# Tails of the shrinking projections as seven half-size products, with their weight sums formed in the third pair

## The reference

```python
x = x + (1.0 + g2)[:, None, :] * conv_ffn(h, ff_w_up[i], ff_conv_w[i], ff_conv_b[i], ff_w_down[i])
...
def rms_norm(x, gain):
    y = xf * lax.rsqrt(jnp.mean(xf * xf, axis=-1, keepdims=True) + RMS_EPS)
```

## Time and profile before

| | us |
|---|---|
| median of 3 runs (lowest, highest) | 2300.97 (2299.34, 2303.53) |
| the profiled execution | 2300.7 |
| its span in the trace | 2298.7 |
| PE busy in it | 2268.2 (99%) |
| DVE busy | 1730.2 (75%) |
| ScalarE busy | 548.3 (24%) |
| mean granted clock of PE | 0.998 |

### The profile page before, as it was taken

The page is one execution under the profiler, slowest core; times in us unless marked ns, Lnnn a source line. Parts: engine busy times, 40 slices in busy tenths (PEclk is TensorE's granted clock), DMA queues, the critical chain, the costliest instruction groups (busy, mean ns, idle before and its releaser), DMA issues.

```text
span 2298.7 us, 45516 instructions
## 1 busy us (share of the span) xinstructions
PE 2268.2 (99%) x18014; PEld 2038.0 (89%) x18014; DVE 1730.2 (75%) x3683; ACT 548.3 (24%) x1388; POOL 184.0 (8%) x296
## 2 busy tenths in 40 slices
PE   8999999999999999999999999999999999999999
PEld 4478999656799997999999799998799998999998
DVE  5866997478579876769986589968769976667883
ACT  2232110027221102213211432212432212213220
POOL 0000011000001010011100011000012100001100
PEclk9999999999999999999999999999999999999999
DMA  6434777751557766468966288674469874456752
GB/s 244 158 129 161 257 276 256 275 186 47 177 202 275 258 257 220 161 218 242 270 234 233 111 233 263 214 262 139 138 202 288 280 260 163 146 173 180 209 179 77
DMA packets 136448, 474.26 MB, mean 206 GB/s; under 512 B 15296, under 2 KB 17472, under 8 KB 135872
## 3 DMA queue, kind: packets, MB, share of 16 engines
q1 hardware_dynamic: 95136, 338.80, 42.2%
q0 software_dynamic: 41120, 132.73, 19.1%
HBM read 470.42 MB, written 1.05 MB: 205 GB/s over the span
## 4 chain that ended last, share of the span: by engine, by line
PE 93%; DVE 5%; ACT 1%; issue 1%; DMA 0%; DVEq 0%; ACTq 0%
PE pair L688 53%; PE bank L688 38%; PE bank L1170 1%; ACT h L1689 1%; PE bank L1000 0%; DVE arena L2955 0%; DVE arena L2995 0%; DVE arena L2991 0%; DVE arena L2363 0%; DVE rstd L2163 0%; DVE arena L3366 0%; PE bank L1111 0%; DVE arena L2438 0%; DMA x<-x_in_dram 0%; DVE h L2172 0%
## 5 line engine op out<-in xcount | busy, mean ns | idle before, releaser
L688 PE MATMUL pair<-arena,ring 128*128 128x128 f32 (+1 forms) x2840 | 389.6, 294 | 3.8 <-issue 2.0
L688 PEld LDWEIGHTS pair<-arena,ring 128*128 128x128 f32 x2840 | 363.6, 192 | 20.0 <-issue 3.6
L688 PE MATMUL bank<-arena 128*128 128x128 f32 (+4 forms) x3172 | 367.0, 278 | 1.9 <-DVE arena L2591 0.8
L688 PEld LDWEIGHTS bank<-arena 128*128 128x128 f32 (+3 forms) x3172 | 348.0, 185 | 16.1 <-issue 6.7
L688 PE MATMUL pair<-arena 128*128 128x128 f32 (+5 forms) x3706 | 340.2, 264 | 2.5 <-DVE arena L2310 1.0
L688 PEld LDWEIGHTS pair<-arena 128*128 128x128 f32 (+4 forms) x3706 | 312.3, 170 | 31.5 <-issue 19.6
L688 PE MATMUL bank<-arena,ring 128*128 128x128 f32 (+1 forms) x2548 | 308.0, 277 | 0.5 <-DVE arena L2363 0.3
L688 PEld LDWEIGHTS bank<-arena,ring 128*128 128x128 f32 x2548 | 295.9, 192 | 3.0 <-DVE arena L2363 0.7
L688 PE MATMUL pair<-h,ring 128*128 128x128 f32 (+1 forms) x2048 | 294.2, 299 | 1.5 <-ACT h L1689 0.9
L688 PEld LDWEIGHTS pair<-h,ring 128*128 128x128 f32 x2048 | 269.9, 192 | 14.6 <-ACT h L1689 1.9
L2758 DVE CUSTOM_DVE_ANT_0 adat<-adat,crow,cols 128x1024 f32<-128x1024 f32 x192 | 243.1, 1277 | 48.0 <-DMA adat<-adaw_dram 48.0
(11 more groups left out here) (320 smaller groups left out, 2460.0 us busy)
## 6 DMA issues: line engine op xcount, KB each, us to landing
ring<-stream_dram SPq DMA_DIRECT2D x638, 512.0 KB, 5.0
adat<-adaw_dram POOLq DMA_DIRECT2D x192, 512.0 KB, 5.3
ring<-stream_dram POOLq DMA_DIRECT2D x80, 256.0 KB, 6.7
arena<-gmrows_dram POOLq DMA_DIRECT2D x1, 2560.0 KB, 11.2
arena<-gmrows_dram POOLq DMA_DIRECT2D x5, 512.0 KB, 9.1
arena<-cmpw_dram POOLq DMA_DIRECT2D x1, 2112.0 KB, 8.6
x<-x_in_dram SPq DMA_DIRECT2D x2, 512.0 KB, 4.5
arena<-mem_in_dram SPq DMA_DIRECT2D x1, 1024.0 KB, 8.8
```

What stands on the lines that cost most here:

```text
L688: return nc.tensor.matmul(out, lhsT, rhs, start=start, stop=stop)
```

## The change

- `tail_pair` replaces the halves in the tail: seven products of K/2 matmuls. The first five give all that the first half of the tokens needs; the last two (the mixed ones, for the second half alone) come last. Their banks are those of the tail's two groups, one late bank, and both banks of the second and of the third pair, for which PE waits.
- `norm_sum(norm, 0)` stands in the sixth product, in front of its matmul j = 5.
- DVE forms four more sums of weights for the tail, in the loop of the third pair. Its modulation tiles, which stood alone in that loop, come behind the four sums and in front of the pair's combination. The first three sums wait for the fourth, fifth and sixth product of the third pair (`down_read`), the fourth for the pair's end (`mm_done`).
- `early_tail` and `late_tail` are the additions to `x`; the latter stands inside `normalise` of the first half, at k = 1 and k = 5. ScalarE copies the tail's first product and squares the second half at k = 5 in place of after k = 7.
- `norm_sum(norm, 1)` stands at k = 4 in place of 3 behind a shrinking projection, where the next one runs in halves.
- In the last norm, the gain's product over the first six tiles comes after `normalise` of the first half.

```diff
@@ plan, tiles_of
+                if kind == "tail":
+                    lin.tail = (at - lin.K * len(ns), group + len(places) - TAIL)
+            counts[grows] += len(lin.pairs) + (not grows)
-            if kind == "pair":
+            if kind in ("pair", "tail"):
@@ names
+                for p in range(len(lin.pairs)):
+                    DOWN_READ.append([("down_read", n_read + r + 1) for r in range(3)] + [("mm_done", lin.g0 + p + 1)])
+                    n_read += 3
+                DOWN_READ.append([("mm_done", lin.g0 + lin.groups)] * 4)
+        def tail_places(g):
+            return [USED[g][0], USED[g + 1][0], LATE[0], *USED[g - 2], *USED[g - 1]]
@@ TensorE, seven
+                def tail_pair(t, g):
+                    own = down_own(name)
+                    places = tail_places(g)
+                    def product(n, stationary, move, free=None, before=None):
+                        for j in range(half_k):
+                            if before is not None and j == 5:
+                                before()
+                            ins = mm(banks[places[n]][:, 0:P], stationary(j), move(j), j == 0, j == half_k - 1)
+                            if j == 0 and free is not None:
+                                release(ins, True, free)
+                        return ins
+                    bank_free(g)
+                    bank_free(g + 1)
+                    product(0, lambda j: tile(t + j), lambda j: moving(2 * j)[:, HALVES[0]], t
+                            ).then_inc(sem("half_done"), 1)
+                    product(1, lambda j: tile(t + 3 * half_k + j), lambda j: sums[:, 3, j, :]
+                            ).then_inc(sem("half_done"), 1)
+                    product(2, lambda j: tile(t + half_k + j), lambda j: moving(2 * j + 1)[:, HALVES[0]]
+                            ).then_inc(sem("half_done"), 1)
+                    pe.wait_ge(sem("freed_dve"), FREER[g - 2][1])
+                    pe.wait_ge(sem("down_summed"), 4 * (lin.pair0 + len(lin.pairs)) + 2)
+                    product(3, lambda j: own[2][:, j, :], lambda j: sums[:, 2, j, :]).then_inc(sem("half_done"), 1)
+                    pe.wait_ge(sem("down_summed"), 4 * (lin.pair0 + len(lin.pairs)) + 4)
+                    product(4, lambda j: own[1][:, j, :], lambda j: sums[:, 1, j, :], t + 2 * lin.K
+                            ).then_inc(sem("half_done"), 1)
+                    pe.wait_ge(sem("freed_dve"), FREER[g - 1][1])
+                    product(5, lambda j: own[3][:, j, :], lambda j: moving(2 * j + 1)[:, HALVES[1]], None,
+                            lambda: norm_sum(norm, 0)).then_inc(sem("mm_done"), 1)
+                    product(6, lambda j: own[0][:, j, :], lambda j: sums[:, 0, j, :]).then_inc(sem("mm_done"), 1)
-                        for i in range(TT):
-                            for at in range(len(ns)):
...
+                        tail_pair(t, g)
@@ h_ready
-                late_k = 3 if PLAN[SOURCE[norm]].kind == "S" else 4
+                late_k = 4
@@ ScalarE, squares
+                if lin.kind == "S":
+                    act.wait_ge(sem("half_done"), HALF[name] + 1)
+                    nc.scalar.copy(ebuf[:, len(lin.pairs) % 2, 7, :], banks[tail_places(lin.tail[1])[0]][:, 0:P]
+                                   ).then_inc(sem("first_copied"), 1)
...
+                        if i == 0 and lin.kind == "S" and k == 5:
+                            last_squares(1)
@@ VectorE, residual
                     for r in range(4):
-                        if p + 1 < len(lin.pairs):
-                            down_weights(name)
-                        if between is not None and r < 3:
+                        down_weights(name)
+                        if between is not None and r < 3 and p + 1 < len(lin.pairs):
                             between(3 * p + r)
+                    for r in range(3 if between is not None and p + 1 == len(lin.pairs) else 0):
+                        between(3 * p + r)
                     e = ebuf[:, p % 2]
                     link(combined(lin.g0 + p, e))
+                def early_tail():
+                    e = ebuf[:, len(lin.pairs) % 2]
+                    p4, p2, p7, p6 = (banks[b][:, 0:P] for b in tail_places(lin.tail[1])[1:5])
+                    dve.wait_ge(sem("first_copied"), FIRST[lin.tail[1]])
+                    corner = chained(plus_row(C, e[:, 7:8, :]))
+                    dve.wait_ge(sem("half_done"), HALF[norm] + 2)
+                    fourth = chained(plus(E, x[:, E, HALVES[0]], p4))
+                    dve.wait_ge(sem("half_done"), HALF[norm] + 3)
+                    after(corner)
+                    plus(C, x[:, C, HALVES[0]], p2).then_inc(sem("x_half"), 1)
+                    add_squares(C - 1, slice(0, TOK), C)
+                    dve.wait_ge(sem("half_done"), HALF[norm] + 4)
+                    mixed = chained(V.tensor_tensor(e[:, 4, :], p7, e[:, 7, :], ALU.add))
+                    after(max(fourth, mixed))
+                    row = chained(plus_row(E, e[:, 4:5, :]))
+                    dve.wait_ge(sem("half_done"), HALF[norm] + 5)
+                    after(row)
+                    plus(E, x[:, E, HALVES[0]], p6).then_inc(sem("x_half"), 1)
+                    add_squares(C, HALVES[0], C + 1)
+                    sixth = chained(plus(C, x[:, C, HALVES[1]], p6))
+                    return sixth, chained(plus(E, x[:, E, HALVES[1]], p6))
+                def late_tail(k):
+                    if k == 1:
+                        dve.wait_ge(sem("mm_done"), lin.tail[1] + 1)
+                        after(late[0])
+                        late[0] = chained(plus(C, x[:, C, HALVES[1]], banks[tail_places(lin.tail[1])[5]][:, 0:P]))
+                    if k == 5:
+                        fifth = banks[tail_places(lin.tail[1])[6]][:, 0:P]
+                        dve.wait_ge(sem("mm_done"), lin.tail[1] + 2)
+                        after(max(late))
+                        plus(C, x[:, C, HALVES[1]], fifth).then_inc(sem("freed_dve"), 1)
+                        plus(E, x[:, E, HALVES[1]], fifth).then_inc(sem("freed_dve"), 1)
+                        add_squares(C, HALVES[1], C + TAIL + 1)
...
+                normalise(norm, gain, 0, late_part if lin.kind == "F" else late_tail)
+                if norm == "final":
+                    gained(0, DK - TAIL)
+                    dve.wait_ge(sem("sq_done"), SQUARES[norm] + DK + TAIL)
+                    gained(DK - TAIL, DK)
                 normalise(norm, gain, 1)
@@ VectorE, down_weights
-                    dve.wait_ge(sem("down_read" if r < 3 else "mm_done"), 3 * (q - 1) + r + 1 if r < 3 else DOWN_GROUP[q - 1])
+                    signal, value = DOWN_READ[q - 1][r]
+                    dve.wait_ge(sem(signal), value)
```

More of the change, by code:

```diff
@@ L524, in build @@
                 SOURCE[f"mix2_{i}"] = f"cdown{i - 1}"
+        ROOTS, SQUARES, ADDED, TAILS, HALF = {}, {}, {}, {}, {}
+        n_root = n_square = n_added = n_tail = n_half = 0
+        for name in NORMS:
+            ROOTS[name], SQUARES[name], ADDED[name], TAILS[name] = n_root, n_square, n_added, n_tail
+            HALF[name] = n_half
+            n_half += 0 if name in WHOLE else 5 if PLAN[SOURCE[name]].kind == "S" else TAIL
+            n_root += 1 if name in WHOLE else TT
+            n_square += DK if name in WHOLE else DK + TAIL
+            n_added += 0 if name in WHOLE else DK - TAIL - 1 + TT
+            n_tail += 0 if name in WHOLE else TAIL
         SPREADS = {}
@@ L552, in build @@
                 n_sums += len(lin.ktiles)
-        DOWN_GROUP = [lin.g0 + p + 1 for lin in PLAN.values() if lin.kind == "S" and not lin.grows
-                      for p in range(len(lin.pairs))]
+        DOWN_READ, n_read = [], 0
+        for lin in PLAN.values():
+            if lin.kind == "S" and not lin.grows:
+                for p in range(len(lin.pairs)):
+                    DOWN_READ.append([("down_read", n_read + r + 1) for r in range(3)] + [("mm_done", lin.g0 + p + 1)])
+                    n_read += 3
+                DOWN_READ.append([("mm_done", lin.g0 + lin.groups)] * 4)
         UP_PAIRS = [(t, g, lin.name) for lin in PLAN.values() if lin.kind == "S" and lin.grows
@@ L572, in down_own @@
             return gm_out_own(name) if name.startswith("gm_out") else downW[name != "down0"]
+        TAIL_GROUPS = [lin.tail[1] for lin in PLAN.values() if lin.kind == "S" and not lin.grows]
+        def tail_places(g):
+            return [USED[g][0], USED[g + 1][0], LATE[0], *USED[g - 2], *USED[g - 1]]
         FIRST = {}
         for g, place in enumerate(USED):
-            if len(place) > 1:
+            if len(place) > 1 or g in TAIL_GROUPS:
                 FIRST[g] = len(FIRST) + 1
@@ L829, in seven @@
                 t, g = lin.tile0, lin.g0
[L831 to L837, removed]
                 grows = lin.grows
@@ L1692, in squares @@
                             last_squares(1)
-                    if i == 0 and (shift is None or lin.kind == "S"):
```

(11 more changed lines are left out.)

19 lines of the change are left out of this document (8 added, 11 removed).

## The result

The changed kernel takes 2316.13 us (median of 4 runs, 2315.23 to 2317.16); the kernel before took 2301.73 beside it (2299.34 to 2303.53). The ratio is 1.0065, 95% interval 1.005 to 1.0079: 14.4 us slower, with 82 matmuls fewer. The profiled execution has a span of 2314.9 us, 16.2 more than before; 1.4 of that had already gone before the first tail, nearly all of it in the first 19 us, where the two programs do the same. So this part is no effect of the change.

What follows compares the result with a forecast made beforehand. TensorE, 93% of the chain, was taken as the bound. Removed matmuls give at most 18.3 us, but waits and seams bring the sum to +8.05: 2309.0 us, own range 2305.6 to 2314, wider range 2299.5 to 2318.

Steps and rivals of the forecast that it cites:

- rival 4: In the five tails with tiles, TensorE's waits bring its clock down: +8.5 us, 2317.5 in total; chance 0.15.
- five tails, DVE's work late: Tiles behind the fourth sum delay combination and additions: 2.46 us saved, 4.5 waited, plus 2.1 each, +10.5 us.
- five tails, the clock: In the five tails with tiles, no clock loss was counted in the forecast's sum: 0 us.
- `gm_out0` with `cup0`: Tail with two tiles and the seam behind it: -1.79 + 0.5 + 0.45 = -0.8 us.
- `gm_out3` with `cup3`: Tail without tiles and the seam behind it: -1.79 + 0.45 = -1.3 us.
- `cdown3` and the end: Tail without tiles saves 2.46 us; the later gain's product at the kernel's end costs 1.3: -1.2 us.
- `hg_f`, `mla_q`: Starts of these two linears: later `norm_sum` costs 0.45 us in the first, later input 0.4 in the second.
- `nsa_in`, behind `down0`: Start of the linear behind this tail: no loss was forecast, 0 us.
- rival 1: Quick refills: both tile refills in the five tails land in 3.4 us, no change, 2300.5; chance 0.2.
- The cover behind `norm_sum`: In the tail, 17 matmuls (3.80 us) behind `norm_sum`, plus its own 0.45, suffice to cover the first `h` tile.
- Rival 2: Combination in the five tails starts before T0 + 6.8 (T0: tail's first matmul), so TensorE never waits: 2286.2; chance 0.08.
- The seams: From tail to next linear: `norm_sum` at k = 4 costs 0.45 us at `cup0`, `cup3`, `hg_f`; `mla_q` 0.4; end 1.3.

Runs made afterwards that it cites:

- Experiment 4: Changed kernel with ten more matmuls, their result unused, in front of `norm_sum` in the five tails with tiles: 2305.19 us, ratio 1.0017.
- experiment 5: Changed kernel with four more matmuls, their result unused, in front of `norm_sum` in the five tails with tiles: 2306.65 us, ratio 1.0026.
- experiment 1: Changed kernel with the third pair's modulation tiles and their loads left out (27 of 192): 2286.94 us, ratio 0.9937.
- experiment 7: Changed kernel, third pair's tiles spread: one behind each of the first three sums, two behind the combination: 2286.59 us, ratio 0.9937.
- experiment 9: Kernel with tiles spread and k = 3, the gain's product over six tiles put before the last norm's first half: 2285.81 us, ratio 0.9934.
- experiment 6: Changed kernel with three more matmuls in front of the sixth product in the five tails with tiles: 2314.22 us, ratio 1.0055.
- experiment 8: Changed kernel with the third pair's tiles spread and the second half's `norm_sum` back at k = 3: 2286.47 us, ratio 0.9936.
- late tiles, old tail: Kernel before the change, with VectorE holding the third pair's tiles until TensorE has ended that pair: 2317.81 us, ratio 1.0067.

## Why the prediction came out as it did

The sign and the place were right, and the cause that was forecast is a real one, but it is only a part of the loss: 2316.1 is 7.1 us above 2309 and outside the forecast's own range of 2305.6 to 2314. It lies in the wider range only because that one took in rival 4 (2317.5). From the offsets and the start of each tail in the two traces, in us:

| step | forecast | measured |
|---|---|---|
| five tails, DVE's work late | +10.5 | +7.0 |
| five tails, the clock | 0 | +9.05 |
| `gm_out0` with `cup0` | -0.8 | -0.45 |
| `gm_out3` with `cup3` | -1.3 | -0.79 |
| `cdown3` and the end | -1.2 | -1.6 |
| `hg_f`, `mla_q` | +0.85 | +1.2 |
| `nsa_in`, behind `down0` | 0 | +0.4 |
| sum | +8.05 | +14.8 |

**The step that failed** is the clock, taken at nothing in the forecast's sum and kept apart as rival 4 at 0.15. What a fall would cost was right (1.7 us each, measured 1.51 to 2.65), and the waits came much as that rival had them: 0.62 to 1.33 us, then 2.33 to 2.64. What failed is the argument against it, that the waits at the start "came one after the other, with little work between". The row was misread. Between the wait of 7.1 us and that of 2.1 us PE worked for 3.59 us:

```profile
7.10 3.59 PE L688 MATMUL bank<-h,cst 128*128 128x256 f32 x8 [7.10 <-DVE h L2842]
```

That is more than the 1.4 us between the two waits of a tail, so the start spoke for rival 4 and not against it. It was weak evidence all the same. The profile after shows the same two waits and a granted clock of 1.00 in both stretches of the earlier trace rows, though PE is 1.3 us later by their end than before; so the clock shown for the first 20 us can't be taken as it stands. Experiment 4 shows the price in the time: 10.9 us, of which the rows of the five tails account for 9.05. The Trainium skill ("TensorE: Matmul & The Clock Gate", "What's actually happening") has the array's clock halved when PE has been idle. The five falls agree with it. That PE has stood still is not enough by itself here: in experiment 5 waits of 1.32 and 1.74 us brought no fall.

**DVE's lateness was mis-sized**, +1.4 us a tail for 2.1. The pieces behind the combination were right: in `cdown1` 3.76 us to the first addition (3.77), 2.16 to the last (2.15), 0.60 to `norm_sum` (0.70). The combination itself came at 10.56 to 10.81 in four tails, and at 11.45 in `down1`, where I had 11.26. In `cdown1` the second landing is the reason, 4.5 us where I took 5.1. So the truth lay between the forecast and rival 1. This error and that of the clock have opposite signs, so that the total is no further off is partly luck; experiment 4, with the clock held, came out at 2305.2, 3.8 below the forecast of a kernel with no clock in it.

**The cover behind `norm_sum`** was right: from there to the next linear it is 4.25 us in experiments 1 and 7 (0.45 + 3.80 in the forecast) and 4.34 behind the wait of experiment 4, and PE does not wait in it. Rival 2 gave 2286.2 and said that it needs some tiles ahead of the last sum. Experiment 7 does that and took 2286.59.

**The seams.** I put all 0.45 us behind `gm_out0` and `gm_out3` down to k = 4. They cost 0.82 each, and behind `gm_out3` k = 3 gives nothing back: the input is late by itself. The tail of `gm_out3` saves 1.61 us (14.74 to 13.13), where I had 1.79. Behind `cdown1` the 0.45 was right: PE's wait for the sums (1.03 us) ended 11.76 us after the start of `hg_f`, now it ends at 12.22, and at 11.88 with k = 3. The rest of the 0.7 there comes later in `hg_f`, and that part varies between kernels with the same seam, so I don't put it down to the change. At the end the reciprocal came 2.66 us after DVE's last addition began, where it was 1.60: +1.1 for my +1.3, of which experiment 9 takes back 0.59. The 0.4 in `nsa_in` I had at nothing. From its start to `down1`'s tail it is 422.91 us before and 423.32 after, but 422.91 to 422.98 in experiments 1, 4, 6, 7, 8 and 9, which have the same seam, and 423.44 in experiment 5. So the seam alone doesn't cost it, and its cause is open.

## What to carry to other kernels

When a stage is given new work on a side engine, look at what stands behind it in that engine's order, and put work with no deadline into the gaps between timed pieces and behind the last piece that someone waits for: here the same tiles in another place turned +14.4 us into -14.6. Cost a wait on TensorE twice, once for its length and once for the clock behind it: 1.5 to 2.7 us for each pair of waits here, where a tail had saved 2.46. And where a wait must stay, a few matmuls without use in it can be worth more than they look, until the wait itself is removed.

## What the runs showed of the hardware

PE's two waits in a tail, and whether the granted clock fell to the 1.2 GHz level behind them, in one profiled execution of each kernel:

| kernel | waits (us) | fell |
|---|---|---|
| ten fillers | 0.63 + 0, 1.00 + 0.10, 0.67 + 0.40, 0.73 + 0.41, 0.69 + 0.41 | no |
| four fillers | 0.45 + 1.44, 0.59 + 1.45, 0.82 + 1.75, 0.90 + 1.75, 1.32 + 1.74 | no |
| late tiles, old tail | 1.27 + 0.72, 1.42 + 0.84, 1.79 + 0.84, 1.64 + 0.84 | no |
| late tiles, old tail | 3.13 + 0.66 | yes |
| changed kernel | 0.67 + 2.33, 1.33 + 2.33, 0.72 + 2.64, 0.62 + 2.63, 0.75 + 2.63 | yes |
| fillers in front | 0 + 2.33, 0.19 + 2.63 | no |
| fillers in front | 0.34 + 2.64, 0.85 + 2.64, 0.99 + 2.34 | yes |

A single wait of 2.33 us left the clock up, and the same wait with 0.67 us of waiting ahead of it, and 1.4 us of work between, brought it down. That suggests that the short first wait counts, but it isn't shown: these are single executions, and the five of the kernel with fillers in front differ among themselves. Shortening the second wait is what the times bear out. Near the edge it goes either way: 0.19 + 2.63 kept the clock and 0.34 + 2.64 did not. The sum of the two waits doesn't decide it either, for 1.32 + 1.74 kept it and 0.67 + 2.33 did not. Each fall behind these waits lasted 3.4 us, or 6.8, and it could begin up to 1.45 us after PE was at work again, so the slow matmuls need not be the first ones behind the wait. What tells the cases at the edge apart, and when it is 3.4 and when 6.8 us, stays open.
